# Modulation's products on four groups of 32 columns, and a later place for layer 1's chunks

## The reference, cut to what matters

```python
def modulation(cvec, w_mod, b_mod):
    m = (jax.nn.silu(cvec) @ w_mod + b_mod)[..., None, :]
    return jnp.split(m, 6, axis=-1)

def trunk_layer(x, cx, c, c_ctx, ...):
    sh1, sc1, ga1, sh2, sc2, ga2 = modulation(c, w_mod, b_mod)
    sh1c, sc1c, ga1c, sh2c, sc2c, ga2c = modulation(c_ctx[None], w_mod, b_mod)
    u = (rmsnorm(x, g_mix) * (1 + sc1) + sh1) @ w_in
    uc = (rmsnorm(cx, g_mix) * (1 + sc1c) + sh1c) @ w_in
    ...   # pooling, gated linear attention (GLA), attention, all over x and cx
    x = x + ga1 * mix
    x = x + ga2 * squared_relu_mlp(rmsnorm(x, g_mlp) * (1 + sc2) + sh2, w_up, w_down)
```

## Time and profile before

| | |
|---|---|
| median of three runs | 2255.1 us |
| the profiled execution's own time | 2255.56 us |
| its span | 2253.8 us |
| mean granted TensorE clock | 0.933 |
| PE, DVE, ACT, POOL busy | 91%, 46%, 38%, 14% |
| moved by DMA | 265.67 MB, mean 118 GB/s |

### The profile page before, as it was taken

One profiled execution on the slowest core, in us unless ns is written; L12 is line 12 of the kernel. 1 busy time (PEld: TensorE's weight loads), 2 busy tenths in 40 slices (PEclk: granted clock), 3 DMA queues, 4 the chain that ended last, 5 costly groups with the idle time before them and its releaser, 6 DMA issues.

```text
span 2253.8 us, 27048 instructions
## 1 busy us (share of the span) xinstructions
PE 2040.1 (91%) x11311; PEld 1655.7 (73%) x11311; DVE 1037.1 (46%) x1559; ACT 865.1 (38%) x1385; POOL 311.9 (14%) x357
## 2 busy tenths in 40 slices
PE   6878999998899999898779996888879999998999
PEld 1744554547788888776669895888869987867997
DVE  1611226524333333554544553775345545565554
ACT  2342235413423323453534443443334444434442
POOL 1200005212122221200011111003110003400000
PEclk9879999989899999999779997999989999989999
DMA  8232334432232233131024553431035555512554
GB/s 273 87 112 95 111 112 150 150 112 93 65 104 94 94 94 94 59 112 47 1 75 151 193 181 103 113 124 44 1 126 180 178 186 167 184 50 94 184 177 144
DMA packets 181157, 265.67 MB, mean 118 GB/s; under 512 B 7526, under 2 KB 102314, under 8 KB 180908
## 3 DMA queue, kind: packets, MB, share of 16 engines
q1 hardware_dynamic: 176452, 255.22, 35.1%
q10 hardware_dynamic: 3464, 5.25, 0.7%
q0 software_dynamic: 1120, 3.48, 0.4%
HBM read 262.89 MB, written 1.05 MB: 117 GB/s over the span
## 4 chain that ended last, share of the span: by engine, by line
PE 78%; DVE 10%; ACT 6%; DMA 2%; issue 2%; POOL 2%; SPq 0%; POOLq 0%; DVEq 0%; ACTq 0%
PE ps L69 75%; PE ps L77 3%; DVE WLO L86 2%; ACT AR L80 2%; DVE AR L96 2%; DVE AR L86 2%; ACT WHI L80 1%; DMA RAW<-in_w_mod_dram 1%; DMA RAW<-in_w_in_dram 1%; POOL XR L86 1%; ACT L80 1%; DVE TL L86 1%; ACT XN L80 1%; POOL SM L86 1%; DVE SM L99 1%
## 5 line engine op out<-in xcount | busy, mean ns | idle before, releaser
L86 DVE TENSOR_TENSOR WLO<-RAW,WHI 128x1024 fp32r<-128x1024 f32 (+1 forms) x402 | 469.6, 1210 | 346.9 <-ACT WHI L80 346.8
L80 ACT ACTIVATE WHI<-RAW 128x1024 fp32r<-128x1024 f32 (+1 forms) x402 | 390.1, 1020 | 323.4 <-PE ps L69 298.4
L69 PE MATMUL ps<-TH,WHI 128*128 128x256 f32 (+1 forms) x1408 | 433.9, 308 | 21.9 <-DVE WLO L86 14.9
L69 PE MATMUL ps<-TH,WLO 128*128 128x256 f32 (+1 forms) x1408 | 431.7, 307 | 0.0
L69 PE MATMUL ps<-TL,WHI 128*128 128x256 f32 (+1 forms) x1408 | 431.7, 307 | 0.0
L69 PEld LDWEIGHTS ps<-TH,WHI 128*128 128x128 f32 x1408 | 275.6, 196 | 34.4 <-issue 19.6
L80 ACT ACTIVATE AR<-ps 128x512 f32<-128x512 f32 (+3 forms) x258 | 122.5, 490 | 422.3 <-PE ps L69 343.0
L69 PEld LDWEIGHTS ps<-TL,WHI 128*128 128x128 f32 x1408 | 275.5, 196 | 10.2
L69 PEld LDWEIGHTS ps<-TH,WLO 128*128 128x128 f32 x1408 | 275.1, 195 | 10.3
L69 PE MATMUL ps<-WHI,TH 128*128 128x512 f32 (+3 forms) x624 | 247.8, 397 | 9.4 <-DVE WLO L86 8.8
L69 PE MATMUL ps<-WHI,TL 128*128 128x512 f32 (+3 forms) x624 | 235.6, 378 | 0.0
(11 more groups left out here) (171 smaller groups left out, 2273.0 us busy)
## 6 DMA issues: line engine op xcount, KB each, us to landing
RAW<-in_w_mod_dram SPq DMA_DIRECT2D x48, 1024.0 KB, 5.1
RAW<-in_ffn_w_in_dram SPq DMA_DIRECT2D x44, 1024.0 KB, 5.1
RAW<-in_w_up_dram SPq DMA_DIRECT2D x32, 1024.0 KB, 5.5
RAW<-in_w_down_dram SPq DMA_DIRECT2D x32, 1024.0 KB, 5.1
RAW<-in_ffn_w_out_dram SPq DMA_DIRECT2D x20, 1024.0 KB, 5.1
RAW<-in_dil_w_in_dram SPq DMA_DIRECT2D x18, 1024.0 KB, 5.0
RAW<-in_gdn_w_in_dram SPq DMA_DIRECT2D x16, 1024.0 KB, 5.7
RAW<-in_w_in_dram SPq DMA_DIRECT2D x12, 1024.0 KB, 5.5
```

The source lines that it names most:

```text
L69: return Made(None if self.eng is None else self.eng.matmul(o, l, r, start=start, stop=stop))
L80: return Made(None if self.eng is None else self.eng.activation(o, i, f, **k))
L86: return Made(None if self.eng is None else self.eng.tensor_tensor(o, a, b, op))
```

## The change

- `SC2` becomes 128 x 32 per block: two columns of the vectors and thirty of zeros. The product of block k of a tile writes partitions 32k to 32k+31, so the four products of a tile go to four groups of 32 columns and each group sums its two blocks of the chunk.
- `act_modulate` copies all 128 partitions of the bank to `ROWS`, now 128 x 512 and single, in the place of `LM` in `CF`; it waits for the turn of m-1 instead of m-2.
- `pe_modturn` is four full products: `ROWS` (128 x 128 each) stationary, `SEL` (128 x 2) moving. `SEL` has ones at the rows that belong to a column, so that the product turns and adds the four groups. DVE makes it from `IDN` at the start, and clears `SC2`.
- The masks `LM` are loaded later, by POOL, behind the last turn in layer 1; the mask helper of the second block waits for them. `HM`, two columns of zeros and ones, is made by memsets and no longer from `LM`.
- Layer 0's attention keeps chunks 4 to 11, layer 0's GLAs have 12 to 15, layer 1's attention has 16 to 19, layer 1's GLAs have 20 to 23. `dve_modend` runs behind chunks 3 and 11 of a layer.
- The cap on splits ahead holds through attention and GLA of both layers.

```diff
@@ -258,7 +257,10 @@
 
         RT = R8[:, 0:512]
         WG = R8[:, 512:1536].rearrange("p (l n) -> p l n", l=2)
-        ROWS = R8[64:66, 0:1024]
+
+        ROWS = CF[:, 1024:1536]
+        SC2 = CF[:, 1536:1792].rearrange("p (k s) -> p k s", k=8)
+        SEL = CF[:, 1792:1794]
         CROW = AR[0:2, 0:1024]
 
         signals = []
...
@@ -436,24 +439,21 @@
                 v = t.of(t.raw)
                 pe.wait_ge(w_land[t.i % NRAW], t.i)
                 for k in range(4):
-                    i = pe.matmul(b[64:66, :], SC2[:, k0 + k, :], v[:, k, :], k0 + k == 0, k0 + k == 7)
+                    i = pe.matmul(b[32 * k:32 * k + 32, :], SC2[:, k0 + k, :], v[:, k, :], k0 == 0, k0 == 4)
                 i.then_inc(pe_gemm, ("used", t.i), ("mod", m))
 
         def act_modulate(m):
             act.wait_ge(pe_gemm, ("mod", m))
-            if m >= 2:
-                act.wait_ge(pe_mod, ("turn", m - 2))
-            h = m % 2
-            act.act(ROWS[:, 512 * h:512 * h + 512], banks.of(("mod", m))[64:66, :], ACT.Copy).then_inc(
-                act_mod, ("free", ("mod", m)), ("row", m))
+            if m >= 1:
+                act.wait_ge(pe_mod, ("turn", m - 1))
+            act.act(ROWS, banks.of(("mod", m)), ACT.Copy).then_inc(act_mod, ("free", ("mod", m)), ("row", m))
 
         def pe_modturn(m):
-            h = m % 2
             b = banks.take(("modt", m), ring)
             wait_free(("modt", m))
             pe.wait_ge(act_mod, ("row", m))
             for i in range(4):
-                o = pe.transpose(b[:, 2 * i:2 * i + 2], ROWS[:, 512 * h + 128 * i:512 * h + 128 * i + 128], IDN[64:66, 64:66])
+                o = pe.matmul(b[:, 2 * i:2 * i + 2], ROWS[:, 128 * i:128 * i + 128], SEL, True, True)
             o.then_inc(pe_mod, ("turn", m))
 
         def dve_modturn(m):
...
@@ -499,8 +499,8 @@
                 yield
                 dve_modturn(m)
                 l, ch = chunks[m]
-                if ch == 11:
-                    dve_modend(l, 4 if l == 0 else 0, 12)
+                if ch in (3, 11):
+                    dve_modend(l, 0 if ch == 3 else 4, ch + 1)
                 yield
 
 
...
@@ -671,7 +671,8 @@
                     act_square("in0", ti, c, 7)
             for m in range(4):
                 act_modulate(m)
-            act.dma(CF[:, 128:2048], T["cf"][:, 128:2048]).then_inc(ld_cf, "cf")
+            act.dma(CF[:, 128:1024], T["cf"][:, 128:1024]).then_inc(ld_cf, "cf")
+            act.dma(CF[:, 1920:2048], T["cf"][:, 1920:2048]).then_inc(ld_cf, "cf")
             act.wait_ge(pe_c, "crow")
             act.dma(AR[:, 2048:3072], T["mu"]).then_inc(ld_mu, "mu")
             act.dma(PMD[:, :], T["pm"]).then_inc(ld_pm, "pm")
...
@@ -682,8 +683,12 @@
         def dve_start():
             dve.memset(R8[0:33, 512:1536], 0.0).then_inc(dve_c, "wz")
             dve.memset(RT[32:33, :], 1.0).then_inc(dve_c, "ones")
+            dve.memset(SC2, 0.0).then_inc(dve_c, "sc0")
+            dve.wait_ge(ld_id, "idn")
+            dve.reduce(SEL, IDN.rearrange("p (g c) -> p c g", g=4)[:, 0:2, :], ALU.add).then_inc(dve_c, "sel")
             dve.wait_ge(pe_c, "crow")
-            dve.copy(SC2, banks.of("crow")[:, 0:16].rearrange("p (k s) -> p k s", k=8)).then_inc(dve_c, ("free", "crow"), "sc")
+            dve.wait_ge(dve_c, "sc0")
+            dve.copy(SC2[:, :, 0:2], banks.of("crow")[:, 0:16].rearrange("p (k s) -> p k s", k=8)).then_inc(dve_c, ("free", "crow"), "sc")
             dve_norm("in0", 0)
             dve_norm("in0", 1)
             for m in range(4):
...
@@ -700,9 +705,10 @@
                     dve_norm("in0", ti + 2, ti)
             dve.wait_ge(ld_mu, "mu")
             dve.copy(MU[:, :], AR[:, 2048:3072]).then_inc(dve_c, "mu")
-            dve.wait_ge(ld_cf, "cf")
-            dve.ts(HM[:, 0:1], LM[:, 6, 0:1], -1.0, 1.0, ALU.mult, ALU.add)
-            dve.copy(HM[:, 1:2], LM[:, 6, 0:1]).then_inc(dve_c, "hm")
+            for x in range(2):
+                dve.memset(HM[0:64, x:x + 1], 1.0 - x)
+                m = dve.memset(HM[64:128, x:x + 1], 1.0 * x)
+            m.then_inc(dve_c, "hm")
             dve_splits(1)
 
         def pool_start():
...
@@ -3002,11 +3009,11 @@
             for g in gs:
                 yield from g
 
-        M1, M2 = range(4, 12), range(12, 24)
-
-        def projections_cap(engine):
-
-            engine.cap = tile_of["w_in", 0, 4, COLS["kv"][0]].j
+        MODS = [(range(4, 12), range(12, 16)), (range(16, 20), range(20, 24))]
+
+        def projections_cap(engine, l):
+
+            engine.cap = tile_of["w_in", l, 4, COLS["kv"][0]].j
 
         def pe_program():
             gring.set(0, 1, 2, 3)
...
@@ -3019,14 +3026,14 @@
                 advance(p, solo(l))
                 ring.set(5, 6, 7)
                 oring.set(4)
-                weave((p, left(l)), (pe_attention(l), souls(l)), *([(pe_mods(M1), 16)] if l == 0 else []))
+                weave((p, left(l)), (pe_attention(l), souls(l)), (pe_mods(MODS[l][0]), 2 * len(MODS[l][0])))
                 grings[0].set(0, 1, 5)
                 grings[1].set(2, 3, 6)
                 ring.set(4, 7)
                 if l == 0:
-                    weave((chain(pe_attended(l), pe_pooling(l)), 8), (pe_gla(l, 0), 28), (pe_gla(l, 1), 26), (pe_mods(M2), 24))
+                    weave((chain(pe_attended(l), pe_pooling(l)), 8), (pe_gla(l, 0), 28), (pe_gla(l, 1), 26), (pe_mods(MODS[0][1]), 8))
                 else:
-                    weave((chain(pe_attended(l), pe_gla(l, 0), pe_pooling(l)), 7), (pe_gla(l, 1), 26))
+                    weave((chain(pe_attended(l), pe_gla(l, 0), pe_pooling(l)), 7), (pe_gla(l, 1), 26), (pe_mods(MODS[1][1]), 8))
                 gring.set(0, 1, 2, 3)
                 ring.set(4, 5, 6)
                 pe_wout(l)
...
@@ -3048,17 +3055,16 @@
         def act_program():
             act_start()
             for l in range(2):
-                if l == 0:
-                    projections_cap(act)
+                projections_cap(act, l)
                 p = act_project(l)
                 advance(p, solo(l))
-                weave((p, left(l)), (act_attention(l), souls(l)), *([(act_mods(M1), 16)] if l == 0 else []))
+                weave((p, left(l)), (act_attention(l), souls(l)), (act_mods(MODS[l][0]), 2 * len(MODS[l][0])))
                 if l == 0:
-                    weave((chain(act_attended(l), act_pooling(l)), 8), (act_gla(l, 0), 28), (act_gla(l, 1), 26), (act_mods(M2), 24))
+                    weave((chain(act_attended(l), act_pooling(l)), 8), (act_gla(l, 0), 28), (act_gla(l, 1), 26), (act_mods(MODS[0][1]), 8))
                     act.wait_ge(dve_gl[1], ("lo", 0, 1))
-                    act.cap = 10 ** 9
                 else:
-                    weave((chain(act_attended(l), act_gla(l, 0), act_pooling(l)), 7), (act_gla(l, 1), 26))
+                    weave((chain(act_attended(l), act_gla(l, 0), act_pooling(l)), 7), (act_gla(l, 1), 26), (act_mods(MODS[1][1]), 8))
+                act.cap = 10 ** 9
                 act_wout(l)
                 act_mlp(l)
             act_final()
...
@@ -3102,6 +3107,8 @@
                     pool.wait_ge(pe_at, ("s", 1, len(UNITS[1]) - 1))
                     pool_row("gdn")
                     run(pool_gla(l, 0), pool_gla(l, 1))
+                    pool.wait_ge(pe_mod, ("turn", 23))
+                    pool.dma(CF[:, 1024:1920], T["cf"][:, 1024:1920]).then_inc(ld_lm, "lm")
                 pool_wout(l)
                 pool_mlp(l)
             pool_final()
```

More of the change, by code:

```diff
@@ L238, in program @@
         CWC = small(96)
-        SC2 = small(16).rearrange("p (k s) -> p k s", k=8)
         MODC = small(192).rearrange("p (l s j k) -> p l s j k", l=2, s=2, j=6)
@@ L269, in signal @@
             return s
-        ld_c, ld_id, ld_x, ld_ctx, ld_small, ld_wg, ld_cf, ld_mu, ld_pm, ld_gf, ld_row, ld_di, st_out = [
+        ld_c, ld_id, ld_x, ld_ctx, ld_small, ld_wg, ld_cf, ld_mu, ld_pm, ld_gf, ld_row, ld_di, ld_lm, st_out = [
             signal(n, 16) for n in ("ld_c", "ld_id", "ld_x", "ld_ctx", "ld_small", "ld_wg", "ld_cf", "ld_mu", "ld_pm",
-                                    "ld_gf", "ld_row", "ld_di", "st_out")]
+                                    "ld_gf", "ld_row", "ld_di", "ld_lm", "st_out")]
         w_land = [signal(f"w_land{i}", 16) for i in range(NRAW)]
@@ L2151, in mask @@
         def mask(engine, did, li, gi):
+            engine.wait_ge(ld_lm, "lm")
             engine.wait_ge(dve_iv, ("n", gi))
@@ L3074, in dve_program @@
             for l in range(2):
-                if l == 0:
-                    projections_cap(dve)
+                projections_cap(dve, l)
                 p = dve_project(l)
                 advance(p, solo(l))
-                weave((p, left(l)), (dve_attention(l), souls(l)), *([(dve_mods(M1), 16)] if l == 0 else []))
+                weave((p, left(l)), (dve_attention(l), souls(l)), (dve_mods(MODS[l][0]), 2 * len(MODS[l][0])))
                 if l == 0:
```

(8 more changed lines are left out.)

## The result

The changed kernel takes 2199.4 us (median of 4) against 2256.4 for the kernel before in the same session: ratio 0.974, 95% interval 0.971 to 0.977. The forecast was 2194, its range 2160 to 2230. The profiled execution took 2201.7 us, its span 2199.9.

What follows compares the result with a forecast made beforehand. TensorE (PE) was taken to bound the kernel, busy 91% of the span. Terms -8 - 34 - 45 + 17 + 6 + 3 = -61 from 2255.6 us gave 2194.6, stated as 2194; range 2160 to 2230.

Steps and rivals of the forecast that it cites:

- A chunk's price: PE time of one modulation chunk: 1.77 us for products plus 1.18 for the turn, 2.95 instead of 7.3.
- The step from pooling's two halves to four groups: Pooling's f32 products overlap in two 64-column halves; assumed four 32-column groups also run at once, 1.72 to 1.77 us a chunk.
- an estimate of 2.2 for four: Alternative microseconds for a chunk's products, from the skill's three-group ratio; would make the summed time some 7 us higher.
- Start, -8: Before the first split product: shorter products close DMA holes, last tile lands at 33 to 34; 8 us saved, bounds 4 to 11.
- Layer 0's attention, -34: Eight chunks each 4.3 us shorter on a dense PE: 34 us saved, bounds 28 to 38.
- they move along: PE's holes in layer 0's attention, from w_in loads queued behind chunk tiles, shift earlier and keep their size, largest 8.72 us.
- Layer 0's GLA, -45: Eight chunks leave, four short ones remain, other engines' limits come up: 45 us saved, bounds 25 to 65.
- Layer 1's attention, +17: Four added chunks cost 12 us on a dense PE, plus one w_in load wait of 5; bounds 0 and 30 on the wait.
- the rival with a stall at each chunk: Layer 1's attention meets four 8 us waits instead of one of 5: +27 us, total 2221; chance 0.12.
- Layer 1's GLA and w_out, +9: Four added chunks, about half hidden in PE holes, cost 6 us; w_out's first split not done ahead costs 3.
- The w_out wait: Layer 1, before w_out's first product: the cap stops its split being done ahead, so PE waits, +3 us.
- Tail, 0: From layer 1's MLP on, second block included: not touched by the change, so no difference.

Runs made afterwards that it cites:

- the experiments with one and two groups: Changed kernel with a tile's four products all in one 32-column group, or alternating between two: 2280.7 us (1.012) and 2223.2 us (0.984) against the kernel before.
- the busy start: Changed kernel plus six unread identity products before each wait for one of the start's eight tiles: 2195.3 us, 0.972 of the kernel before.
- the seven with this start: Profiles of the changed kernel and six variants that leave its start code as it is; their start stage took 58.9 to 61.7 us.
- late-chunks kernel: Changed kernel with chunks 16 to 23 all beside layer 1's GLA, none beside its attention: 2181.7 us, 0.966 of the kernel before.
- the experiment: Changed kernel whose twelve chunks beside the attentions read resident constants instead of loading weight tiles: 2161.6 us, 0.957 of the kernel before.

## Why the prediction was right, and where its terms were off

- **A chunk's price.** 1.77 for the products and 1.18 for the turn, 2.95 together; measured 1.92 to 1.93 and 0.95 to 1.05 at the upper clock, about 2.95 (17 of the 20 chunks behind the start have such products, 15 of the 20 such turns). The group's busy time, forecast near 45, is 57.5: the start's eight tiles take 1.93 or 1.94 each, 15.5 us in all, at the lower level, which that figure had left out. The step from pooling's two halves to four groups holds, by the experiments with one and two groups. The friction is greater than I took (1.93 for an ideal of 1.72), and the turn cheaper; that the two errors cancel to 2.95 is luck. The Trainium skill's ratio for three groups (TensorE: Matmul & The Clock Gate, section Why this matters for your kernels), 2.38 or 79% of three, had made an estimate of 2.2 for four; the runs show 91% of ideal for four, and the measurement decides. The Trainium skill (same page, section Part 2) marks the fourth quadrant's bus as not supported; no run here shows such a limit for products in the fourth group.
- **Start, -8: the term that failed; it was -3.3.** Two parts. The last tile landed at 37.9, not at 33 to 34: I had taken 380 GB/s for the stream behind 18 us, and from there to 37.9 it moved 312 on average, with holes left. The length of a tile's products isn't what holds it back: with the busy start eight of them take 1.07 instead of 1.93, and the last tile lands at 36.9 and 38.5 in its two profiles, no earlier than in the seven with this start, where its products begin at 36.7 to 38.3. What does is open. In those seven the start is 2.9 to 5.7 shorter than before: no profile reached 8. And behind the landing the products, two turns and the transposes ran at the lower level, where I had allowed one us: from the last tile's first product to the first split product 23.4 us in the changed kernel and 21.7 in the late-chunks kernel, whose tile and first turn take 1.07 and 1.05.

  PE in order of time of that kernel:

```profile
37.37 1.07 PE L69 MATMUL ps<-RAW,CF 128*32 128x512 f32 x8 [1.95 <-DMA RAW<-in_w_mod_dram]
38.37 1.05 PE L69 MATMUL ps<-CF 128*128 128x2 f32 x8
40.26 1.84 PE L69 MATMUL ps<-CF 128*128 128x2 f32 x8 [0.84 <-ACT CF L80]
```

- **Layer 0's attention, -34: -34.1.** Products 56.8 to 15.9 us in it, turns up; and the holes stayed, as argued, though not quite at their size: 8.72 and 7.30 before, 10.02 and 8.79 after, and one of 5.17 before a turn came in. In the earlier trace rows's stretch PE's busy time fell by 38.9 us and its idle time rose by 4.9, so that the term fits to 0.1 is in part luck. What I didn't see is that these holes are the chunks' own: I wrote that they move along, and left it there, where the experiment puts 29.6 of 220 us on the chunks' loads.
- **Layer 0's GLA, -45: -41.8.** Its parts were forecast at 35.7, 48 and 56.9 and took 33.8, 49.0 and 60.9. DVE in the levels is 38.0 of 49.0 us, 78% busy where I took 83. The tail was short by 4: it runs at a granted clock of 0.64.
- **Layer 1's attention, +17: +17.6.** By its two terms, too: 12 for the work (12.9 measured) and one wait of 5 (4.6). ACT waits once for a w_in tile there, 4.11 us, so the rival with a stall at each chunk is out.
- **Layer 1's GLA and w_out, +9: +1.3.** Mis-sized. The w_out wait came (2.86 us of idle PE before its first product), but in a GLA whose end moved little; with four chunks there it took 90.6 to 94.4 us over four profiles, against 89.4 and 89.8 in the two without: 1 to 5 us.
- **Tail, 0: +6.0.** No instruction differs. In the thirteen profiles it took 1068 to 1078 us. The place is some 320 us into it. The window there, kernel before:

```profile
1504.00:1555.00 51.00, 47.19 (x287) 42.44 (x286) 29.48 (x53) 16.18 (x25) 16.56 (x11) 0.90 0.24 81
```

The same work in the changed kernel:

```profile
1444.00:1499.00 55.00, 51.50 (x289) 46.75 (x290) 29.61 (x53) 16.26 (x26) 16.58 (x11) 0.81 0.22 73
```

  PE's busy time is up by 4.3 us at a granted clock of 0.81 for 0.90. The same stage took 1068.4 and 1071.6 us in two other kernels with the change's code, so I take it to go with the execution; no two profiles of one kernel show it. It and the start's 4.7 and the GLA's 3.2 on the one side, and the 7.7 of layer 1's GLA on the other, make 6 of the 7 us between -61 and -53.9.

The total was close partly since these errors cancel; the four large terms (attention and GLA of layer 0, attention of layer 1, a chunk's price) each hold by themselves.

## What to carry to other kernels

A product with few columns is worth splitting over groups of 32 columns, whose four lanes work side by side; price it by the cadence of one lane, and add what it takes to sum the groups. Then ask anew where the work stands, since what was too long to hide may be short enough: here the same chunks cost 6.3 us each beside a dense attention and about half a us (3.6 and 4.4 us for eight, where profiles of the same stage differ by as much) beside a stage whose PE waits on other engines, until that stage is full. Where work brings its own transfers, count the load that must wait for its buffers and queue behind them: in layer 0's attention that was more than half of the price (29.6 of 50.6 us), in layer 1's a quarter, and it shows as idle time of PE and not in what the chunk keeps busy.

## What the runs showed of the hardware

- Four f32 products in four groups of 32 columns overlap nearly fully, in one PSUM bank and into rows 0 to 127 of it, when they stand one behind the other in program order: 1.93 us for sixteen of 512 columns, 3.63 with two groups, 7.05 with one.
- Where PE gets holes its granted clock is lower, and its work takes longer: the same 807 instructions of layer 0's attention take 140.2 us of PE at 0.89, with three holes of 5 to 10 us, and 134.2 at 0.96 without them.
- A 1 MB load asked for right behind two others on the same queue lands later: the three w_in tiles behind a chunk's two in layer 0's attention took 9.1, 9.3 and 9.9 us from issue to landing, and those without a chunk's loads before them 5.3.
- The granted clock in the profile's windows doesn't tell the level at the start. It reads 1.00 from 16 to 20 us in the changed kernel, where eight products of a tile take 1.93 us, all that PE does in that window, and 1.00 with the busy start, where they take 1.07. The changed kernel:

```profile
16.00:20.00 4.00, 1.93 (x8) 0.20 (x8) 0.87 (x2) 3.74 (x12) 2.23 (x7) 1.00 1.02 328
```

  By the durations the first is the lower level (1.2 GHz) and the second the upper (2.4 GHz).
